# A hybrid trunk layer with PEER experts on one core: gathered rows taken out of the last score stage, and gates that begin earlier

## The reference

```python
def peer(h, w_query, sub_keys, expert_u, expert_v):
    q = jnp.einsum('btd,dhk->bthk', h, w_query).reshape(B, T, PEER_HEADS, 2, PEER_DKEY // 2)
    s = jnp.einsum('bthpk,hpnk->bthpn', q, sub_keys)
    sv, si = lax.top_k(s, PEER_TOPK)
    cand = (sv[..., 0, :, None] + sv[..., 1, None, :]).reshape(...)
    cidx = (si[..., 0, :, None] * PEER_NKEYS + si[..., 1, None, :]).reshape(...)
    best, pos = lax.top_k(cand, PEER_TOPK)
    eidx = jnp.take_along_axis(cidx, pos, axis=-1)
    gates = jax.nn.softmax(best, axis=-1)
    ...
        act = jax.nn.gelu(jnp.einsum('nd,ned->ne', hx, expert_u[ix]))
        return jnp.einsum('ne,ned->nd', act * gx, expert_v[ix])
```

## Time and profile before

| | |
|---|---|
| median of three timed runs | 4934.61 us |
| the profiled execution | 4941.91 us |
| its span, first to last instruction | 4940.1 us |
| TensorE busy | 4705.5 us (95%) |
| VectorE busy | 3028.3 us (61%) |
| GpSimd busy | 1729.0 us (35%) |
| `scores` for 384 tokens, about | 3056 to 3235 us |
| `experts`, about | 3235 to 4940 us |
| moved by DMA in the whole | 1666.68 MB, 337 GB/s |

### The profile page before, as it was taken

The page is one execution under the profiler, slowest core; times in us unless marked ns, Lnnn a source line. Parts: engine busy times, 40 slices in busy tenths (PEclk is TensorE's granted clock), DMA queues, the critical chain, the costliest instruction groups (busy, mean ns, idle before and its releaser), DMA issues.

```text
span 4940.1 us, 54839 instructions
## 1 busy us (share of the span) xinstructions
PE 4705.5 (95%) x22501; PEld 3528.9 (71%) x22501; DVE 3028.3 (61%) x4386; ACT 578.6 (12%) x1080; POOL 1729.0 (35%) x1113
## 2 busy tenths in 40 slices
PE   4989999998999999999999997999999999999998
PEld 1777446444999644446655543699999999999998
DVE  1441006887667576525777757988875447886553
ACT  1521001441222100000000001010000000000000
POOL 0131001674555465411344434433332223342221
PEclk7999999999999999999999998999999999999999
DMA  9918898996222698998899997679999999999996
GB/s 390 383 64 328 317 343 330 366 392 275 95 85 91 253 384 328 391 391 324 330 420 420 414 413 291 234 282 412 417 410 411 396 397 408 415 412 420 403 420 241
DMA packets 237725, 1666.68 MB, mean 337 GB/s; under 512 B 28274, under 2 KB 32770, under 8 KB 37700
## 3 DMA queue, kind: packets, MB, share of 16 engines
q0 software_dynamic: 130048, 939.72, 47.3%
q1 hardware_dynamic: 98884, 673.84, 34.7%
q10 hardware_dynamic: 8544, 49.62, 2.5%
HBM read 1643.31 MB, written 18.94 MB: 336 GB/s over the span
## 4 chain that ended last, share of the span: by engine, by line
PE 39%; DMA 10%; DVE 3%; issue 1%; POOL 1%; ACT 0%; POOLq 0%; DVEq 0%; ACTq 0%
PE ps L242 22%; PE ps L2336 15%; DMA arena_sb<-peer_v,arena_sb 6%; DMA arena_sb<-peer_u,arena_sb 3%; POOL arena_sb L350 1%; PE ps L2279 1%; DVE arena_sb L401 1%; PE ps L1748 1%; DVE arena_sb L396 0%; DMA arena_sb<-peer_vt 0%; PE ps L1969 0%; DVE arena_sb L2525 0%; DVE arena_sb L1682 0%; DMA arena_sb<-w_out 0%; DVE arena_sb L1685 0%
## 5 line engine op out<-in xcount | busy, mean ns | idle before, releaser
L242 PE MATMUL ps<-arena_sb 128*128 128x224 f32 (+3 forms) x9728 | 2296.8, 397 | 4.4 <-PEq L553 2.4
L242 PEld LDWEIGHTS ps<-arena_sb 128*128 128x128 f32 x9728 | 1675.2, 192 | 619.4 <-issue 334.4
L401 DVE SCALAR_TENSOR_TENSOR arena_sb<-arena_sb 128x2048 f32<-128x2048 f32 x412 | 989.6, 2402 | 419.8 <-DMA arena_sb<-peer_v,arena_sb 392.8
L396 DVE CUSTOM_DVE_ANT_0 arena_sb<-arena_sb 128x2048 f32<-128x2048 f32 x416 | 963.5, 2332 | 335.1 <-DMA arena_sb<-peer_u,arena_sb 334.1
L350 POOL DMA_INDIRECT arena_sb<-peer_v,arena_sb x416 | 670.3, 1611 | 1064.7 <-DVE arena_sb L401 875.6
L350 POOL DMA_INDIRECT arena_sb<-peer_u,arena_sb x416 | 632.8, 1521 | 838.0 <-DVE arena_sb L396 406.9
L2336 PE MATMUL ps<-arena_sb 128*128 128x224 f32 x4096 | 776.6, 353 | 1.6 <-ACT arena_sb L2375 0.6
L2336 PEld LDWEIGHTS ps<-arena_sb 128*128 128x128 f32 x4096 | 774.4, 190 | 2.6 <-issue 1.0
L1571 PE MATMUL ps<-arena_sb 128*128 128x512 f32 x768 | 344.6, 607 | 20.6 <-PEq L2642 7.8
L1571 PEld LDWEIGHTS ps<-arena_sb 128*128 128x128 f32 x768 | 146.7, 194 | 213.9 <-issue 196.5
L1748 PE MATMUL ps<-arena_sb 128*128 128x512 f32 x640 | 276.5, 593 | 5.7 <-DMA arena_sb<-w_out 3.5
(11 more groups left out here) (279 smaller groups left out, 2883.4 us busy)
## 6 DMA issues: line engine op xcount, KB each, us to landing
arena_sb<-peer_ut SPq DMA_DIRECT2D x128, 1024.0 KB, 9.3
arena_sb<-peer_vt SPq DMA_DIRECT2D x128, 1024.0 KB, 9.2
arena_sb<-w_mod POOLq DMA_DIRECT2D x64, 1024.0 KB, 8.6
arena_sb<-w_qkv SPq DMA_DIRECT2D x48, 1024.0 KB, 8.9
arena_sb<-w_out SPq DMA_DIRECT2D x48, 1024.0 KB, 7.6
arena_sb<-w_query SPq DMA_DIRECT2D x48, 1024.0 KB, 7.9
arena_sb<-w_mod SPq DMA_DIRECT2D x32, 1024.0 KB, 9.1
arena_sb<-w_ga_r SPq DMA_DIRECT2D x32, 1024.0 KB, 7.7
```

What stands on the lines that cost most here:

```text
L242: mm = pe.matmul(out, weights[:, k * P:(k + 1) * P], x[:, k, :], start=(k == 0), stop=(k == chunks - 1))
L396: nc.vector.tensor_tensor_reduce(rows, rows, total, 1.0, 0.0, ALU.mult, ALU.add, seg.dots[:, p:p + 1]).then_inc(t.rows_used, 1)
L401: nc.vector.scalar_tensor_tensor(out=total, in0=rows, scalar=seg.weight[:, p:p + 1], in1=total, op0=ALU.mult, op1=ALU.add).then_inc(t.rows ...
```

## The change

The last score stage uses 4 rows instead of 29, all of them ahead of the first head. In the first u stretch the gates begin at place 8 instead of 13 and stand two tiles apart, instead of seven tiles for four. `closing[0]` goes from 61 to 63 with it, and `turn_keys` goes from place 11 to place 6. ScalarE's `near` and `soften`, the last steps of the scores, go from places 4 and 7 to 2 and 4. The 25 rows are dealt to `experts`, by a new helper `pace(steps, rows)` that spreads `rows` evenly over `steps` places.

```diff
-    behind = take(t, [10, 3, 3, 2, 3, 3, 3, 2, 0] if nb == 3 else [0 if ctx else 4] + [0] * H, 4 if nb == 3 else 3)
+    behind = take(t, [4] + [0] * H if nb == 3 else [0 if ctx else 4] + [0] * H, 4 if nb == 3 else 3)
...
-    starts = [[13 + 7 * g // 4 for g in range(GROUPS)], [6 + 2 * g for g in range(GROUPS)]]
+    starts = [[8 + 2 * g for g in range(GROUPS)], [6 + 2 * g for g in range(GROUPS)]]
...
-    counts = [0] * 7 + [2, 2, 2, 1] * 14 + [2] + [1, 1, 2, 1, 1, 2, 1, 1, 2, 1] * 6 + [1, 1, 2, 1] + [2, 2, 2, 2, 2, 2, 2, 2, 2, 1] * 6 + [2] * 4 + [1, 1, 1, 1, 2] * 12
+    def pace(steps, rows):
+
+        return [(i + 1) * rows // steps - i * rows // steps for i in range(steps)]
+
+    counts = [0] * 5 + pace(59, 105) + pace(64, 92) + pace(64, 117) + pace(61, 88)
...
+                if h == 0 and s == 2:
+                    t.near(act, H - 2)
                 if h == 0 and s == 4:
-                    t.near(act, H - 2)
-                if h == 0 and s == 7:
                     t.soften(act)
```

## The result

The changed kernel is slower, by 0.44%. The median of five timed runs is 4955.43 us (4951.59 to 4960.26), against 4934.61 us (4929.95 to 4938.24) before: ratio 1.0044, 95% interval 1.0030 to 1.0057. The prediction had 4952 us. The profiled execution took 4960.26 us, its span is 4958.4 us.

A forecast was written before the change was run, and what follows sets the result against it. Experts was taken as bound by TensorE and DMA at once. Last stretch about +20 us, with -6 contained, 18 taken: span 4958 instead of 4940.1, thus 4952 against the median 4934.61; range 4928 to 4971.

The forecast's parts named there:

- a row more of head start: Last stretch: head start may be a row more than counted, so 18 of the about 20 us were taken.
- Score stage at nothing: Last score stage: 25 rows less on VectorE give TensorE, busy throughout, nothing; term 0.
- Tail of the scores: End of the scores: weights there at about 3269, no wait at turn_keys, rows start 19 us earlier.
- First gates: First gates of the first u stretch: the 2.69 us wait and what follows go away, -5.5 us.
- End of the first u stretch: Into the first v stretch: new waits for VectorE's settling (about 3684) and the first v tile (3678.4), together about +5 us.
- First v stretch: First v stretch: slack used up, 74 rows in 321 us at 4.33 us each, about 3 rows outstanding at its end.
- First gates of the second u stretch: Start of the second u stretch: rows 3 late, so TensorE waits 11 us instead of 6.45.
- Later waits of the second u stretch: Second u stretch after its first gates: of 12.7 us of waits and slow spells about 11 go.
- the -6: Sum up to the last stretch: about -6 us, so it starts at 4526 instead of 4532.
- Last stretch: At turn(2): 8.2 rows left, TensorE waits 24 us for join(0), plus a 2.8 us slow spell; about +20 us.
- The ceiling: DMA limit: 435 GB/s fabric ceiling, at which a row beside a tile would cost about 4.0 us; forecast used 4.33.
- the rows keep up: Rival 1: joins done when TensorE reaches turn(2), needing 8 more rows in time; about -11 us, 4924; chance 0.20.

The follow-up runs named there:

- e12: The changed kernel with only the gates put back to their old places, near and soften staying early; stage time 1731.4 us, ratio to before 1.0073.
- e2: The changed kernel with 14 of the last stretch's 64 weight tiles loaded by half only, 7 MiB less; stage time 1707.4 us, ratio to before 1.0005.
- e1: The changed kernel with join(0) and join(1) ten places earlier in the last stretch; stage time 1711.8 us, ratio to before 1.0028.
- e3: The changed kernel with 18 rows instead of 4 in the score stage, 67 instead of 81 in the last stretch; stage time 1703.9 us, ratio to before 0.9995.
- e5: The kernel before with only the change's row lists, gates, near and soften staying where they were; stage time 1752.0 us, ratio to before 1.0107.
- e9: e7 with four rows fewer in the first u stretch (101) and two more in each of the next two; stage time 1691.0 us, ratio to before 0.9972.
- e11: The changed kernel with 27 rows in the score stage and 102, 87, 114 in the next three stretches; stage time 1689.9 us, ratio to before 0.9975.
- e10: The changed kernel with 29 rows in the score stage and 101, 87, 114 in the next three stretches; stage time 1695.6 us, ratio to before 0.9995.
- e4: The kernel before with only the change's gates and earlier near and soften, all 29 rows in the score stage; stage time 1713.5 us, ratio to before 1.0017.
- e7: The changed kernel with 25 rows in the score stage and 105, 87, 114 in the next three stretches; stage time 1689.0 us, ratio to before 0.9976.

## Why the prediction was right

The mechanism and its place came out as forecast, and so did the size of the decisive wait. One step on the way did not, and one term was hit by luck. The sum of the terms was 20.9 us (-5.9 + 24 + 2.8), of which 18 were taken; measured are 23.3 us of stage time and 20.8 between the medians, so the deduction for a row more of head start wasn't borne out.

- **Score stage at nothing: right.** From line 1809 to `experts` it takes 208.0 us before and 208.3 after.
- **Tail of the scores, no wait at `turn_keys`: right.** The first row starts 34.5 us into the stage instead of 52.6, 18.1 earlier (forecast 19).
- **First gates, no wait there: right** as to the wait. But the cause was put in the wrong place: in e12, with the gates where they were, the wait is 0.8 us too, and the v stretch starts 3672.96 - 3232.32 = 440.6 us into the stage, against 439.7 after and 445.3 before. Rows that start earlier, and the early weights, do all of it that stands clear of the noise.
- **End of the first u stretch: the step that failed.** The prediction had VectorE's settling at about 3684 and the first v tile at 3678.4, and +5 us. Measured, TensorE waits 1.1 us, and the v stretch starts 439.7 us into the stage instead of 445.3: 5.6 earlier. The prediction left the price of the 98 rows as it was and put the five new ones at 3.96 us. Before, 98 rows lie between 3287.90 and 3682.85, 4.03 us each; after, 103 rows between 3264.79 and 3669.30, 3.93 each, while that stretch moves 420 GB/s instead of 413. A tenth of a microsecond over some 100 rows are the 10 us. And the first v tile was there 7.2 us after SP's start (3662.80), not 10.
- **First v stretch: right in kind.** GpSimd waits for VectorE, at 420 GB/s. The window of 321 us has 76.5 rows (113 instructions on line 396, halved, and 20 on line 401), 4.2 us each where 4.33 was taken: 2.5 rows more than the 74 forecast. The prediction missed one row of before: its window has 138 instructions on VectorE, 137 of line 396 and one of line 401, so 69.5 rows and 4.62 us each.
- **First gates of the second u stretch: right, a little larger.** 14.2 us instead of 11. By the prediction's terms the gates step would stand 892 us into the stage (882.7 before, +5, and 11 - 6.45 more of wait), and TensorE would come to it at 881. The step stands at 884.8 and TensorE came at 870.6: the rows were 7 us sooner and TensorE 10 to 11, so more of what was left became a wait.
- **Later waits of the second u stretch: right in sign, smaller.** From the first gates to the last it takes 4498.73 - 4115.08 = 383.7 us instead of 391.4: 7.7 us won where 11 were forecast. At turn(2) TensorE is 4.8 us ahead of before; 5.9 were forecast. **That this term came out is luck.** The prediction's own parts give -1.5 (+5, +4.5 and -11), and the -6 came from a count of rows beside them; the measured parts are -5.6, +7.8 and -7.7. What was off in the parts made good what the sum lacked.
- **Last stretch: right.** The settling of place 191 stands 4540.41 - 3230.30 = 1310.1 us into the stage, 3.6 sooner than forecast. The rows cost 5.0 us (28 in 141 us), then 4.4 (38 in 169) and 4.3 (11 in 47), where 5.2 and 4.33 were taken, and 9 are left when TensorE stands still, where 8.2 were forecast. These cost 2.9 us each, at 361 GB/s, and not 2.5. The wait is 26.1 us where 24 stood, with 2.0 us of low clock where 2.8 stood.
- **The ceiling.** The Trainium skill ("DMA: Bandwidth & Descriptors", Specifications) gives 435 GB/s for the fabric. The trace agrees as far as it goes: the best of the windows shown is 422 GB/s (3670 to 3748), and a row in the v stretch cost 4.2 us, not the 4.0 that was estimated from that page. Its 358 GB/s for HBM were passed in all windows shown up to turn(2).

Of the rivals, the one on the other side (the rows keep up) needed 8 rows more in time. The v stretch gave 2.5 of them, and the last stretch took them back: from 4664 to 4833 a row cost 4.4 us and not 4.33, and TensorE came to turn(2) 1650.3 us into the stage where 1649.2 were forecast. So 9 rows were left instead of 8.2. e2 shows how near it was: 7 MiB less for the DMA, and the wait is 7.4 us.

What is shown: the loss is at turn(2) (e1), it is DMA time (e2), it goes when rows go back into the scores (e3), and it is there with the gates at either place (e5, e12). What stays open: why the first v tile is 2.4 to 3.9 us late in e9 to e11. The traces narrow it. SP starts it as soon as the last gates step is over, in all four kernels (in e9 that step ends at 3658.11 + 1.89 = 3660.00, and SP starts at 3660.04). From there to the start of the v stretch it takes 9.6 us in e9, 9.9 in e10 and 8.5 in e11 instead of 7.2. So the transfer is slower, and its start isn't late; what slows it wasn't tried.

## What to carry to other kernels

In a program that fills two resources at once in one stage and only one in another, a piece of work is worth the bandwidth of the stage in which it runs: 25 rows cost nothing to keep in a stage that ran DMA at 67%, and some 4 us of DMA time each in one at 100%. The time of the kernel shows less of it, 1.7 us a row in e3, for it pays only for the rows that make a step late for which the bound engine waits. Look for that step at the end of the stage too: here a wait of 14 us on the way was there with and without the loss (e3). Before moving a step forward (the gates), ask what has to be ready for it: here the place of `near` and `soften` was worth 20.6 us once the rows waited for them, and that of the gates too little to be read from two stage times.

## What the runs showed of the hardware

A wait of TensorE has a second price behind it. The first pass of the first v stretch has the same 1024 matmuls in every kernel. Behind waits of 0.65 to 1.86 us it took 193.94 to 193.97 us; behind 1.94 us (e4) and 2.40 us (e11) 195.63 each; behind 3.55 us (e9), 3.85 us (e10) and 7.83 us (e7) 196.75, 196.66 and 196.36. The window with the 14.2 us wait at the first gates of the second u stretch (4069 to 4112, after) has a mean granted clock of 0.92, against 1.00 around it. Right behind the wait the granted clock is 0.50 (4115.0 to 4118.8), which is the lower of the two levels, 1.2 instead of 2.4 GHz, and the 16 matmuls there took 3.67 us where they take 1.89 undisturbed. Behind the wait of 3.55 us in e9 it is 0.50 too (3669.6 to 3673.0), and behind the 1.09 us of the changed kernel it stays at 1.00 (3669 to 3672). So a wait of about 2 us costs nearly as much again, a longer one adds little beyond that (2.4 to 2.8 us behind 3.55 to 7.83 us ahead of this pass, 2.0 behind the 26.1 us at turn(2), and 4132.55 - 4115.08 - 13.89 = 3.6 behind the 14.2 us at the gates, after), and the shorter waits ahead of this pass cost nothing beyond their length. Ahead of gates steps they do cost a little: in e4 two steps behind waits of 0.7 us stand 14.88 us apart, thus 14.16 without the wait, where 13.89 is the undisturbed period; in e9 a wait of 2.6 us there cost 3.2 more.

With DMA at a share of 1.01 the GB/s still differed between stretches, from 406 (before, 4532 to 4673) to 422 (after, 3670 to 3748), with the share unchanged. The share says that the engines were occupied, and not that nothing more would fit: after a change look at the GB/s beside it.
